# ScalarE instead of VectorE copies the value blocks of an attention layer out of PSUM

## The reference, cut to what matters

```python
q  = (rms_norm(q_lat, q_a_norm_w) @ w_q_b).reshape(B, S, N_HEADS, QK_DIM)
kv = (rms_norm(kv_lat, kv_a_norm_w) @ w_kv_b).reshape(B, S, N_HEADS, QK_NOPE_DIM + V_HEAD_DIM)
k_nope, v = kv[..., :QK_NOPE_DIM], kv[..., QK_NOPE_DIM:]
k = jnp.concatenate([k_nope, k_rope_h], axis=-1)
q = rms_norm(q, q_norm_w)
k = rms_norm(k, k_norm_w)
```

## Time and profile before

| | us |
|---|---|
| median of 3 runs | 1953.79 |
| lowest and highest run | 1953.61, 1955.35 |
| the profiled execution, its own time | 1954.56 |
| its span in the trace | 1952.8 |

### The profile page before, as it was taken

The page is one execution under the profiler, slowest core; times in us unless marked ns, Lnnn a source line. Parts: engine busy times, 40 slices in busy tenths (PEclk is TensorE's granted clock), DMA queues, the critical chain, the costliest instruction groups (busy, mean ns, idle before and its releaser), DMA issues.

```text
span 1952.8 us, 22534 instructions
## 1 busy us (share of the span) xinstructions
PE 1553.3 (80%) x9834; PEld 870.0 (45%) x9834; DVE 558.9 (29%) x1106; ACT 244.6 (13%) x574; POOL 46.5 (2%) x30
## 2 busy tenths in 40 slices
PE   9999999886656676568899999998857566565777
PEld 6687688432222232223365787884313122222323
DVE  3554782211111121123335546612111111111212
ACT  3242210200000000001122431102000000000000
POOL 0300000000000000000003000000000000000000
PEclk9999999988888788789999999999978788887888
DMA  7532055799999999999972225277999999999998
GB/s 301 209 115 87 1 214 233 281 381 437 430 426 439 427 431 434 431 429 431 426 319 86 87 96 206 103 307 306 437 434 432 433 430 428 432 430 432 431 425 372
DMA packets 28222, 643.89 MB, mean 330 GB/s; under 512 B 3040, under 2 KB 4576, under 8 KB 7392
## 3 DMA queue, kind: packets, MB, share of 16 engines
q1 hardware_dynamic: 26960, 638.41, 77.5%
q10 hardware_dynamic: 1168, 4.07, 0.5%
HBM read 641.42 MB, written 1.05 MB: 329 GB/s over the span
## 4 chain that ended last, share of the span: by engine, by line
PE 51%; DMA 45%; DVE 2%; DVEq 1%; issue 1%; ACT 0%; SPq 0%; ACTq 0%
DMA region<-w_down_dram 42%; PE ps L1077 11%; PE ps L637 7%; PE ps L700 6%; PE ps L831 6%; PE ps L897 3%; PE ps L1004 2%; DMA ring<-w_gbu_dram 2%; PE ps L663 2%; PE ps L814 1%; PE ps L678 1%; PE ps L803 1%; DMA region<-w_down_last_dram 1%; PE ps L542 1%; PE ps L605 1%; PE ps L742 1%
## 5 line engine op out<-in xcount | busy, mean ns | idle before, releaser
L1004 PE MATMUL ps<-ring,region 128*32 128x384 f32 (+1 forms) x2842 | 287.3, 534 | 178.0 <-DMA ring<-w_gbu_dram 178.0
L1077 PE MATMUL ps<-region,late 128*32 128x512 f32 x1320 | 215.9, 778 | 149.9 <-DMA region<-w_down_dram 146.2
L1004 PEld LDWEIGHTS ps<-ring,region 128*32 128x32 f32 x2842 | 118.1, 124 | 338.4 <-DMA ring<-w_gbu_dram 196.7
L1077 PEld LDWEIGHTS ps<-region,late 128*32 128x32 f32 x1320 | 57.3, 139 | 287.5 <-issue 283.3
L637 PE MATMUL ps<-xnT,ring 128*128 128x256 f32 x768 | 175.2, 382 | 4.7 <-DVE region L1479 2.9
L1881 DVE TENSOR_TENSOR region<-region,ps 128x256 f32<-128x256 f32 x32 | 13.5, 421 | 515.6 <-PE ps L1004 515.6
L637 PEld LDWEIGHTS ps<-xnT,ring 128*128 128x128 f32 x768 | 142.7, 190 | 32.2 <-issue 5.7
L1893 DVE COPY region<-ps 128x512 f32<-128x512 f32 x30 | 20.7, 691 | 343.6 <-PE ps L1077 343.6
L1101 PE MATMUL ps<-region 128*128 128x512 f32 x208 | 100.4, 615 | 19.4 <-issue 19.4
L1004 PE MATMUL ps<-region 128*32 128x384 f32 (+1 forms) x1224 | 102.5, 463 | 1.5 <-DMA region<-w_ga_dram 1.5
L700 PE MATMUL ps<-xnT,ring 128*128 128x256 f32 x384 | 86.3, 380 | 0.0
(11 more groups left out here) (263 smaller groups left out, 1545.6 us busy)
## 6 DMA issues: line engine op xcount, KB each, us to landing
region<-w_down_dram SPq DMA_DIRECT2D x28, 5632.0 KB, 32.4
ring<-w_gbu_dram SPq DMA_DIRECT2D x28, 4928.0 KB, 33.4
region<-w_ga_dram SPq DMA_DIRECT2D x14, 6336.0 KB, 36.9
ring<-w_ga_dram SPq DMA_DIRECT2D x11, 6336.0 KB, 36.0
ring<-units_dram SPq DMA_DIRECT2D x26, 2048.0 KB, 8.5
region<-units_dram SPq DMA_DIRECT2D x8, 2048.0 KB, 12.1
ring<-w_ga_dram SPq DMA_DIRECT2D x2, 4288.0 KB, 20.7
ring<-w_ga_dram SPq DMA_DIRECT2D x4, 2112.0 KB, 10.2
```

The source lines that it names most:

```text
L1004: m = mm(bank(b, QW[j], rows=CAP, row0=CAP * j), xs[:, i, q * CAP:(q + 1) * CAP], row[:, c0:c0 + QW[j]], start=i == 0, stop=i == DB - 1)
L1077: m = mm(bank(c, rows=CAP, row0=CAP * j), hT[:, b * P + CAP * j:b * P + CAP * (j + 1)], wd[:, CT * b + j, c * 512:(c + 1) * 512], start=b ...
```

## The change

ACT gets the copies of the four value blocks of each layer; DVE keeps the four key copies. The semaphore `kv_dve` (eight per layer) is replaced by `k_dve` and `v_act` (four per layer each), and PE waits for both before block 2. On ACT the value copies stand ahead of the squares of the same half's key.

```diff
@@ PE
                     if g < 6:
                         pe.wait_ge(s["q_act"], L * 6 + g + 1)
                     else:
-                        pe.wait_ge(s["kv_dve"], L * 8 + g - 5)
+                        pe.wait_ge(s["k_dve"], L * 4 + g - 5)
...
-                pe.wait_ge(s["kv_dve"], (L + 1) * 8)
+                pe.wait_ge(s["k_dve"], (L + 1) * 4)
+                pe.wait_ge(s["v_act"], (L + 1) * 4)
@@ ACT
                 for t in range(SB):
-                    act.wait_ge(s["kv_dve"], L * 8 + 4 * t + 2)
+                    for c in range(2):
+                        g = 4 * t + 2 + c
+                        act.wait_ge(s["kv_psum"], L * 8 + g + 1)
+                        af(v_t[:, t, c * 512:(c + 1) * 512], bank((3 + g % 6) % 7), ACT.Copy).then_inc(s["v_act"], 1)
+                    act.wait_ge(s["k_dve"], L * 4 + 2 * t + 2)
                     af(ksq[:, t], k_nope[:, t], ACT.Square).then_inc(s["ksq_act"], 1)
@@ DVE
                 for g in range(8):
                     t, c = g // 4, g % 4
-                    dve.wait_ge(s["kv_psum"], L * 8 + g + 1)
-                    src = bank((3 + g % 6) % 7)
                     if c < 2:
-                        m = copy(k_t[:, t, c * 512:(c + 1) * 512], src)
-                    else:
-                        m = copy(v_t[:, t, (c - 2) * 512:(c - 1) * 512], src)
-                    m.then_inc(s["kv_dve"], 1)
+                        dve.wait_ge(s["kv_psum"], L * 8 + g + 1)
+                        copy(k_t[:, t, c * 512:(c + 1) * 512], bank((3 + g % 6) % 7)).then_inc(s["k_dve"], 1)
```

More of the change, by code:

```diff
@@ L261, in build @@
         norm1_rms r_dve r2_dve xT_psum xw_dve xw_act r_psum xnT_dve lat_psum lat_rms lat_ready latT_psum latT_dve latT_act
-        filt_psum arg_dve sin_act q_psum q_act kv_psum kv_dve ksq_act qkss_dve qkrms_act qw_pool kw_pool rqk_dve qkr_pool qkw_scaled qk_ready
+        filt_psum arg_dve sin_act q_psum q_act kv_psum k_dve v_act ksq_act qkss_dve qkrms_act qw_pool kw_pool rqk_dve qkr_pool qkw_scaled qk_ready
         proj_psum conv_act conv_dve
```

## The result

The changed kernel took 1956.7 us (median of 22 runs, 1952.99 to 1959.14) against 1953.62 us for the one before (22 runs, 1951.44 to 1956.15). The ratio is 1.0015, with a 95% interval from 1.0009 to 1.0021: about 2.9 us slower by the ratio (3.1 by the medians), less than 0.2%, but no chance result. The forecast was 1955.4, with 1.64 us of loss. The measured loss is nearly twice that, and its mechanism is only half of what happened. The profiled execution took 1956.16 us, with a span of 1954.3.

A forecast was written before the change was run, and what follows sets the result against it. The prediction took PE's wait before block 5, set by the reciprocal and DVE/POOL turns, as the bound. Two layers of +0.82 us gave +1.64: 1953.79 + 1.64 = 1955.43, stated as 1955.4 us, range 1953.0 to 1957.4.

The forecast's parts named there:

- The place: PE's wait before block 5, set by the reciprocal through DVE/POOL turns, decides; its idle grows from 1.46 to 2.3-2.4 us.
- The value copy on ACT: Last value copy before block 2: 0.59 us on ACT against 0.69 on DVE, so block 2 could start 0.10 earlier.
- The square and POOL: Late second key square puts POOL's second L468 over DVE's 32-column add, L1638; the add ends 0.82 us late per layer.
- the 0.02 taken from L1528: L1528, a four-column DVE add, ended 0.02 us behind POOL's L452; the hold of L1638 was forecast from it.
- the 0.1 that the prediction allowed on top for the hand-over: Upper bound on L1638's hold: the whole of POOL's L468 plus 0.1 us for the hand-over.
- the sum's term, 1.64: Delay from DVE and POOL taking turns ahead of block 5: 0.82 us in each of two layers, +1.64 us.
- The step that failed: Argument against a clock fall: clock 1.00 from 79.4 to 84.6 despite 1.46 us idle before block 5.
- rival C: PE's clock falls behind the router or before block 5: 3.4 us more, 1958.8; slower by over 0.2%; chance 0.06.
- Rival A: No hold of DVE's add L1638 by POOL: each layer gains 0.12 us, giving 1953.55; chance 0.10.
- Rival B: Expert stream hides part of the delay at each layer's end; at half, the time is 1954.6; chance 0.08.
- Rival D: Clock gives back: layer 0's low stretch behind the router shrinks to layer 1's length, giving 1953.7; chance 0.06.
- the sum's basis: Whole-kernel time before the change: profiled execution 1954.56 us, 0.77 above the runs' median 1953.79; 1.64 was added to each.

The follow-up runs named there:

- e1: The changed kernel with each half's key square moved ahead of that half's two value copies on ACT; 1950.45 us, ratio 0.9984 to the kernel before.
- e2: The kernel before, DVE making all copies, with ACT's second key square waiting for all eight copies instead of six; 1957.94 us, ratio 1.0022.
- e5: The changed kernel with two unused 512-column matmuls per layer on PE ahead of the wait for block 5; 1954.22 us, ratio 1.0007 to the kernel before.
- e9: e1 with layer 0's square-root table load moved from behind the last value copy into ACT's earlier idle time; 1950.22 us, ratio 0.9980 to the kernel before.
- e6: The changed kernel run again unaltered, on the same chip as e5; 1956.26 us, ratio 1.0016 to the kernel before.

## Why the prediction was right, and where it fell short

- *The place.* That the wait before block 5 decides, and not the one before block 2, held: idle time 2.34 us against the 2.3 to 2.4 forecast. The reciprocal sets it through the turns that POOL and DVE take, though in the trace of before the chain of waits leads to the conv of block 2. e1 shows it from the other side.
- *The value copy on ACT.* 0.60 us against 0.69, forecast 0.59. Of the 0.10 only half arrived: PE's wait before block 2 is 0.73 instead of 0.78.
- *The square and POOL.* Since this profile's L678 starts 0.15 later, the square (68.61), L468 (69.74) and L476 (73.47) are where they were forecast (68.50, 69.63, 73.34) within 0.04. L1639 ends 0.05 behind POOL's product, between the 0.02 taken from L1528 and the 0.1 that the prediction allowed on top for the hand-over; no run shows that 0.1 for this add (e2 has 0.06). Per layer the turns cost 21.34 - 20.48 = 0.86 from block 2 on; as block 2 starts 0.05 sooner, 0.81 of it reaches the transposes, against 0.82. So the sum's term, 1.64, measured 1.62, and e5, where nothing else is left, lies at +0.9 by its medians and +1.4 by its ratio.
- *The step that failed* is the evidence against rival C: "the clock is 1.00 from 79.4 to 84.6 with 1.46 us idle". That row says nothing of 2.34 us, and the longer gap was itself named as a place for the fall. The mechanism was real and its chance far too small. It cost 1.69 us in a layer in which it struck, half of the 3.4 us that I priced it at, so that it did not by itself carry the result over 0.2%, and the range held. The forecast of 1.64 us is short of the measured 2.9 us by 1.3. The six profiles with the long gap show 8 falls, 1.3 an execution, which would be 2.3 us; the interval of the ratio (1.8 to 4.1 us of loss) leaves 0.1 to 2.5 us for the clock, so how often it falls is known only roughly.
- *Rival A* (no hold) is refuted by L1639's row. *Rival B* (half of a shift lost in the expert part) was not tested by itself, but e1 and e9 speak against it: their rows show the transposes earlier by 3.0 and 3.6 us over both layers, and their ratios give 3.1 and 3.9. For a delay it is less well known; e5 has 1.6 us in its rows, and its interval reaches from a gain of 0.4 to a loss of 3.1. (That PE mostly waits in the expert part, as said at the start, is too strong: from 390 to 1000 us in the trace of before it is busy for 429 of 610.) *Rival D* stays open: the clock around the router differs between executions of one and the same kernel (from 384 to 386 us it was granted 1.00 in the changed kernel and 0.50 in e6), and no run here separates a shift of it.
- *A word on the sum's basis.* The profiled executions differ by 1956.16 - 1954.56 = 1.60 us, which looks like the forecast. It is not: the stretch of the change accounts for 0.81 + 2.50 = 3.3 us in that pair, and the expert part in between happened to be 2.8 us shorter. The agreement was luck.

What stays open: why the clock falls in layer 1 each time and in layer 0 seldom. The idle time is the same, and so are PE's rows for the 25 us ahead of it (L678 for 13.90, idle 0.73, L637 for 10.60 in both layers of the changed kernel); further back the work of PE is not (layer 0 has had the filter's matmuls, layer 1 comes from the expert part). This was not tried.

## What to carry to other kernels

When work is moved to an idle engine, look at what stands behind it in that engine's order. Here the copies were free and the square behind them was not, and swapping the two turned a loss of 2.9 us into a gain of 3. An instruction of 0.19 us on VectorE took 1.15 us beside a GpSimd product, so list what else runs in the new place of a shifted instruction. And price a longer idle time of TensorE twice: once as itself, and once as a fall of its clock. A row with a shorter gap is no evidence against such a fall.

## What the runs showed of the hardware that was not expected

- A scalar add of 16 columns from SBUF to SBUF on VectorE, twice, took 1.27 us beside a GpSimd product and 0.36 without; reductions of 1024 columns took 1.22 us beside it and 1.21 without.
- Idle gaps of TensorE of up to 1.78 us never lowered the granted clock at this place (five kernels, both layers, three of the ten cases without any gap); gaps of 2.18 to 2.78 us did so in 8 of 12 cases, each time for about 3.4 us by the mean clock of the windows, which delayed the transposes by 1.5 to 1.7 us where a layer without the fall is there to compare.
- Two matmuls without use in a gap of 2.34 us kept the clock at 1.00 in both layers of the one execution that was profiled.
